# A drain behind every fourth gather of the second expert table

## The chip, the cores and the metric

The kernel runs on one core of a Trainium2 chip. The metric is device time in microseconds (us), the median over several runs. A profile is one further execution, recorded by the hardware profiler; its own time stands beside the median below.

## What is computed

Two transformer-like blocks run one after the other on a sequence of 256 tokens of width 1024, all in float32. The change lies in the last part of the first block, a mixture of very many small experts. Each token is routed, by eight heads that pick 16 experts each, to 128 out of 16384 experts; an expert is one row of a first table `u` and one row of a second table `v`. Cut to that part:

```python
def expert_chunk(args):                     # 128 tokens at a time
    xc, ic, gc = args                       # tokens, expert numbers, gates
    u = jnp.take(u_tab, ic, axis=0)
    a = jnp.einsum('chkd,cd->chk', u, xc)   # one dot product per token and expert
    wgt = gc * jax.nn.gelu(a)
    vv = jnp.take(v_tab, ic, axis=0)
    return jnp.einsum('chk,chkd->cd', wgt, vv)
```

`ic` differs from token to token, so the rows have to be gathered from HBM. The second block (a state-space mixer, a linear recurrence and a feed-forward part) follows on the result.

## The kernel before

The 256 tokens are two tiles of 128, one token on each partition. For a tile the kernel walks through the 128 choices of its tokens: step e (0 to 255 over both tiles) takes, for every token, its choice number e. One step needs two gathers, one from each table, of 128 rows of 1024 float32 numbers, 512 KB each. So there are 512 gathers.

All of them are issued by GpSimd, as indirect DMAs. `gather_u(e)` (line 687) fills one of 5 slots with rows of the first table, `gather_v(e)` (line 701) one of 7 slots with rows of the second. Before it reuses a slot, GpSimd waits: `gather_u(e)` for the flag `dot_ready` of step e - 5, `gather_v(e)` for the flag `pair_summed`, which counts pairs of steps, up to the pair that holds step e - 7. Behind a wait the gather is issued, and its landing raises a semaphore of the slot (`u_full`, `v_full`). The order is written out by hand: step 0 of both tables, step 1 of the first, and then the loop below, in which the first table runs one step ahead.

The other engines consume in order. VectorE takes the dot product of a slot of the first table with the token (`dot_expert`, line 2489), ScalarE turns it into a weight and spreads that on a diagonal matrix (`weigh_expert`, lines 1737 to 1746), and TensorE multiplies the diagonal with the slot of the second table and adds up in PSUM (`sum_expert`, line 1143, two matmuls for each step). Into the same stretch the program folds other work: queries, scores and the routing of the later choices, and projections of the second block's input. The weights for these are loaded by SP on its own queue.

Before that stage GpSimd sets up constants (lines 637 to 675: memsets, iota, small selections and sums) with drains among them; behind the stage it issues a few plain DMAs (lines 718 to 730).

```python
            gather_u(0)
            gather_v(0)
            gather_u(1)
            for e in range(1, TT * EXPERTS):
                if e + 1 < TT * EXPERTS:
                    gather_u(e + 1)
                gather_v(e)
```

Of the kernel before, what the change touches and what calls it, by code (L numbers as in the profile page):

```python
# [244 lines left out]
def pairs(experts):  # L245

    return (experts + 1) // 2


def build(nc, T, out):  # L250

    with ExitStack() as ctx:
# [195 lines left out]
        def flag(name):  # L448

            if name not in S_:  # L450
                S_[name] = sem(name)
            return S_[name]

        def group_wait(eng, name, i):
            g = (name, i)
            eng.wait_ge(bank_full[GROUP_BANK[g]], GROUP_USE[g] + 1)
# [52 lines left out]
        def turn_wait(eng, *u):  # L509

            eng.wait_ge(turned, turn_no[u] + 1)
# [40 lines left out]
        def _(sp):  # L552
            second_halves = []
            for c, (_, w, k0, kt, col, n) in enumerate(CHUNKS):
                b = BEFORE[c]
                if c == FRONT:
# [79 lines left out]
        def _(pool):  # L636
# [41 lines left out]
            def gather_u(e):  # L678

                r, k, slot = e // ROUTE, e % ROUTE, e % NU  # L680
                if e in FIRST_IDX:
                    pool.wait_ge(flag("idx_ready"), FIRST_IDX.index(e) + 1)
                elif e == TOPK or (k == 0 and r):
                    pool.wait_ge(flag("idx_ready"), route_step(e) + len(FIRST_IDX))
                if e >= NU:
                    pool.wait_ge(flag("dot_ready"), e - NU + 1)
                pool.indirect_dma_start(  # L687
                    u_rows[:, slot, :], None, T["peer_u"],
                    bass.IndirectOffsetOnAxis(ap=expert_idx[:, r % 2, k:k + 1], axis=0),
                ).then_inc(u_full[slot], 16)  # L690

            def gather_v(e):

                r, k, slot = e // ROUTE, e % ROUTE, e % NV
                if e >= NV:
                    pool.wait_ge(flag("pair_summed"), pairs(e - NV + 1))
                if e == 0:
                    turn_wait(pool, "m", 1, 0)
                if e == 3:
                    group_wait(pool, "out1", 1)  # L700
                pool.indirect_dma_start(  # L701
                    v_rows[:, slot, :], None, T["peer_v"],
                    bass.IndirectOffsetOnAxis(ap=expert_idx[:, r % 2, k:k + 1], axis=0),
                ).then_inc(v_full[slot], 16)

            gather_u(0)
            gather_v(0)
# [5 lines that stand above are left out]
# [2468 lines left out]
```

## Time and profile before

| what | us |
|---|---|
| median of 3 runs | 1311.55 (1310.23 to 1312.46) |
| span of the profiled execution | 1366.9 |
| GpSimd busy in it | 500.2 |
| TensorE matmuls busy in it | 1199.9 |
| VectorE busy in it | 861.8 |
| ScalarE busy in it | 420.2 |

The profiled execution is 55 us longer than the median; times read from its trace are compared with its own span. A gather's record on GpSimd covers its issue; the movement of its bytes by the 16 DMA engines isn't part of that record and is seen by when the first user of the slot starts.

### The profile page before, as it was taken

The page shows a single profiled execution, that of the slowest core. Times are in us where ns is not written, and L with a number is a line of the kernel's source. Part 1 is how long each engine was busy: PE and PEld are TensorE (multiplying, and loading weights), DVE is VectorE, ACT ScalarE, POOL GpSimd, SP SyncE. Part 2 cuts the span into 40 slices and gives each one's busy share as a digit, 9 for nine tenths or more (in the row PEclk, how much of TensorE's full clock was granted, in tenths as well). Part 3 has the DMA queues.
Part 4 walks back from the last instruction along what each step waited for, and adds up shares of the span by engine and source line. Part 5 has one row for each costly group of instructions (what it writes and reads, how often), then busy time and mean ns, then how long its engine had stood idle before and what let it go on. Part 6 is the DMA issues. An engine that isn't in the chain of part 4 may idle for free. (4 is left out here: it accounts for less than half of the span.)

```text
span 1366.9 us, 14592 instructions
## 1 busy us (share of the span) xinstructions
PE 1199.9 (88%) x4663; PEld 665.4 (49%) x4663; DVE 861.8 (63%) x1765; ACT 420.2 (31%) x1138; POOL 500.2 (37%) x580
## 2 busy tenths in 40 slices
PE   7899888888778978876788889789999999999997
PEld 4676554433344542222345433236544545999443
DVE  2657669574663654776746557679989543676345
ACT  2213334344223343343423324432323311222000
POOL 1000356666665666766666666630000000000000
PEclk9999999999998999999999999999999999999999
DMA  9998789999998999999999999986644444454450
GB/s 358 390 349 326 286 319 339 367 357 367 364 366 300 406 403 405 407 377 364 340 371 353 400 405 409 377 306 233 224 139 148 145 150 156 157 175 145 175 184 31
DMA packets 134303, 405.66 MB, mean 297 GB/s; under 512 B 10153, under 2 KB 11585, under 8 KB 133971
## 3 DMA queue, kind: packets, MB, share of 16 engines
q0 software_dynamic: 75024, 273.19, 53.1%
q1 hardware_dynamic: 57860, 127.48, 25.8%
q10 hardware_dynamic: 1342, 4.06, 0.8%
q8 instruction: 38, 0.62, 0.2%
q14 instruction: 39, 0.31, 0.1%
HBM read 403.12 MB, written 1.05 MB: 296 GB/s over the span
## 5 line engine op out<-in xcount | busy, mean ns | idle before, releaser
L1143 PE MATMUL psum<-gathered,modr 128*128 128x512 f32 x1024 | 505.0, 633 | 130.3 <-DMA gathered<-in_peer_v_dram,expert_idx 49.0
L2489 DVE CUSTOM_DVE_ANT_0 gathered<-gathered,psum 128x1024 f32<-128x1024 f32 x256 | 311.5, 1217 | 202.3 <-DMA gathered<-in_peer_u_dram,expert_idx 153.3
L1143 PEld LDWEIGHTS psum<-gathered,modr 128*128 128x128 f32 x1024 | 190.7, 199 | 404.7 <-issue 284.9
L687 POOL DMA_INDIRECT gathered<-in_peer_u_dram,expert_idx x256 | 244.9, 957 | 240.5 <-DVE expert_idx L1997 144.0
L701 POOL DMA_INDIRECT gathered<-in_peer_v_dram,expert_idx x256 | 242.6, 947 | 169.9 <-remote 73.7
L780 PE MATMUL psum<-featT,weight_ring 128*128 128x128 f32 (+2 forms) x960 | 145.3, 305 | 14.4 <-issue 11.3
L780 PEld LDWEIGHTS psum<-featT,weight_ring 128*128 128x128 f32 x960 | 133.7, 196 | 43.9 <-issue 35.6
L780 PE MATMUL psum<-weight_ring,featT 128*128 128x512 f32 x336 | 147.9, 596 | 1.3 <-ACT featT L1563 0.8
L1737 ACT ACTIVATE gel<-dots 128x1 f32<-128x1 f32 x256 | 51.1, 200 | 255.1 <-issue 128.1
L1746 ACT ACTIVATE modr<-ident,wgt 128x128 f32<-128x128 f32 x256 | 102.8, 402 | 18.5 <-issue 1.1
L780 PEld LDWEIGHTS psum<-weight_ring,featT 128*128 128x128 f32 x336 | 62.6, 190 | 78.8 <-issue 76.6
L1741 ACT ACTIVATE wgt<-gel,expert_gate 128x1 f32<-128x1 f32 x256 | 75.4, 294 | 17.9 <-issue 0.3
L1989 DVE TENSOR_TENSOR work<-work 128x1088 f32<-128x1088 f32 (+5 forms) x87 | 68.6, 801 | 9.6 <-issue 2.8
L725 POOL DMA_DIRECT2D gathered<-in_b_in_dram x6 | 5.3, 942 | 138.6 <-ACT gathered L1585 104.2
L1585 ACT COPY work<-psum 128x128 f32<-128x128 f32 x32 | 8.4, 262 | 81.5 <-remote 44.6
L1978 ACT ACTIVATE work<-work,pack 128x256 f32<-128x256 f32 x28 | 12.7, 500 | 56.8 <-DVE work L1989 56.8
L1989 DVE TENSOR_TENSOR vectors<-weight_ring 128x1024 f32<-128x1024 f32 x14 | 16.5, 1220 | 20.9 <-PE psum L1512 20.9
L1563 ACT COPY featT<-psum 128x512 f32<-128x512 f32 (+1 forms) x24 | 12.4, 554 | 55.0 <-PE psum L752 53.8
L780 PE MATMUL psum<-weight_ring,uT 128*128 128x512 f32 x64 | 28.2, 593 | 1.0 <-ACT gathered L1585 1.0
L1989 DVE TENSOR_TENSOR gathered<-gathered,psum 128x256 f32<-128x256 f32 (+1 forms) x17 | 8.6, 511 | 29.8 <-PE psum L780 24.9
L1473 PE MATMUL psum<-featT,weight_ring 128*128 128x128 f32 x224 | 27.3, 275 | 0.0
L1473 PEld LDWEIGHTS psum<-featT,weight_ring 128*128 128x128 f32 x224 | 26.1, 192 | 0.0
(443 smaller groups left out, 1343.1 us busy)
## 6 DMA issues: line engine op xcount, KB each, us to landing
weight_ring<-in_w_in_dram SPq DMA_DIRECT2D x16, 2048.0 KB
weight_ring<-in_w_up_dram SPq DMA_DIRECT2D x8, 2048.0 KB
weight_ring<-in_w_down_dram SPq DMA_DIRECT2D x8, 2048.0 KB
weight_ring<-in_ada_w_dram SPq DMA_DIRECT2D x5, 2048.0 KB
work<-in_ada_w_dram SPq DMA_DIRECT2D x5, 2048.0 KB, 16.3
weight_ring<-in_peer_wq_dram SPq DMA_DIRECT2D x3, 2048.0 KB
gathered<-in_ada_w_dram SPq DMA_DIRECT2D x2, 2048.0 KB, 14.5
gathered<-in_peer_u_dram,expert_idx POOLq DMA_INDIRECT x256
```

Source lines behind the costliest of these rows:

```text
L687: pool.indirect_dma_start(u_rows[:, slot, :], None, T["peer_u"], bass.IndirectOffsetOnAxis(ap=expert_idx[:, r % 2, k:k + 1], axis=0),).the ...
L701: pool.indirect_dma_start(v_rows[:, slot, :], None, T["peer_v"], bass.IndirectOffsetOnAxis(ap=expert_idx[:, r % 2, k:k + 1], axis=0),).the ...
L780: last = pe.matmul(psum[0:m, bank, 0:n], lhs(k), rhs(k), start=(k == 0), stop=(k == kt - 1))
L1143: mm = pe.matmul(psum[:, SUM_BANK + half, :], diag[:, e % 8, :], v_rows[:, slot, 512 * half:512 * (half + 1)], start=(e % EXPERTS == 0), s ...
L1473: last = pe.matmul(psum[:, UP_BANKS * (n % 2) + bank, at:at + P], a(g, m), b(g), start=(g == 0), stop=(g == 3))
L1563: ins = act.activation(dst, src, func, **kw) if func else act.copy(dst, src)
L1737: act.activation(gel[:, col:col + 1], dots[:, col:col + 1], ACT.Gelu_apprx_tanh)
L1741: act.activation(wgt[:, col:col + 1], gel[:, col:col + 1], ACT.Copy, scale=expert_gate[:, r % 2, k:k + 1])
L1746: act.activation(diag[:, e % 8, :], ident[:, :], ACT.Copy, scale=wgt[:, col:col + 1]).then_inc(flag("diag_full"), 1)
L1978: act.activation(ffT[:, k, :], ffT[:, k, :], ACT.Relu, bias=pk("b_up")[:, k:k + 1])
L1989: return dve.tensor_tensor(o, a, b, op)
L2489: dve.tensor_tensor_reduce(u_rows[:, slot, :], u_rows[:, slot, :], h2_rows[t], 1.0, 0.0, ALU.mult, ALU.add, dots[:, col:col + 1])
```

## The change

Behind every fourth gather of the second table (steps 3, 7, 11 and so on) GpSimd executes a drain. Nothing else in the program differs.

```diff
@@ -702,6 +702,8 @@
                     v_rows[:, slot, :], None, T["peer_v"],
                     bass.IndirectOffsetOnAxis(ap=expert_idx[:, r % 2, k:k + 1], axis=0),
                 ).then_inc(v_full[slot], 16)
+                if e % 4 == 3:
+                    pool.drain()
 
             gather_u(0)
             gather_v(0)
```

## Rows read from the trace of the kernel before

**Rows 1.** The head of the page: the span of the execution.

```profile
span 1366.9 us, 14592 instructions
```

**Rows 2.** Table of stretches: from:to, length, busy us (instructions) of each engine, clock, DMA.

```profile
core 0: us, PE busy (x) PEld busy (x) DVE busy (x) ACT busy (x) POOL busy (x), PEclk, DMA share, GB/s
152.00:907.00 755.00, 614.61 (x1827) 295.48 (x1825) 476.65 (x1150) 280.76 (x874) 487.42 (x512) 0.95 0.98 371
```

**Rows 3.** GpSimd's timeline: start, duration, instruction, [idle time before it <- what ended it].

```profile
326.33 0.94 POOL L701 DMA_INDIRECT gathered<-in_peer_v_dram,expert_idx  x1 [3.23 <-remote]
327.57 0.94 POOL L687 DMA_INDIRECT gathered<-in_peer_u_dram,expert_idx  x1 [0.30 <-issue]
328.82 0.94 POOL L701 DMA_INDIRECT gathered<-in_peer_v_dram,expert_idx  x1 [0.30 <-issue]
...
335.05 0.94 POOL L687 DMA_INDIRECT gathered<-in_peer_u_dram,expert_idx  x1 [0.30 <-issue]
...
343.76 0.94 POOL L701 DMA_INDIRECT gathered<-in_peer_v_dram,expert_idx  x1 [0.30 <-issue]
```

**Rows 4.** Line 687, all instructions: ns min/median/max, first and last start in us.

```profile
L687 POOL DMA_INDIRECT gathered<-in_peer_u_dram,expert_idx x256: 934/941/1484, 152.0 to 902.3; - x128
```

**Rows 5.** The chain that ended last, at the stage's end: start, duration, what.

```profile
904.90 7.71 DMA gathered<-in_peer_v_dram,expert_idx
...
912.66 2.00 PE psum L1143 x4
```

**Rows 6.** GpSimd's waits in the stage: us in total, times, longest.

```profile
POOL gathered L701 <- remote: 73.7, 29, 4.2
POOL gathered L687 <- issue: 72.9, 228, 1.4
POOL gathered L701 <- issue: 67.5, 215, 2.3
POOL gathered L701 <- PE psum L1143: 28.7, 12, 8.7
POOL gathered L687 <- DVEq L2491: 23.6, 27, 4.4
```

**Rows 7.** VectorE's timeline in the stretch of rows 3: dot products.

```profile
333.05 1.22 DVE L2489 CUSTOM_DVE_ANT_0 gathered<-gathered,psum 128x1024 f32<-128x1024 f32 x1 [2.10 <-DMA gathered<-in_peer_u_dram,expert_idx]
...
341.39 1.22 DVE L2489 CUSTOM_DVE_ANT_0 gathered<-gathered,psum 128x1024 f32<-128x1024 f32 x1 [1.31 <-DMA gathered<-in_peer_u_dram,expert_idx]
```

**Rows 8.** GpSimd's timeline in its opening; drains before lines 649, 661, 667 and 671.

```profile
2.07 0.14 POOL L644 IOTA iota<- 128x16 f32 x1
2.15 1.11 POOL L647 MEMSET inv_freq<- 128x1 f32 x32
3.47 0.29 POOL L649 TENSOR_SCALAR_AFFINE_SELECT ident<-ident 128x128 f32<-128x128 f32 x1 [0.21 <-issue]
...
4.21 0.28 POOL L657 TENSOR_SCALAR_AFFINE_SELECT causal<-causal 128x128 f32<-128x128 f32 x1
4.62 1.14 POOL L661 MEMSET quarter_rows<- 1x128 f32 x4
...
6.70 0.65 POOL L667 TENSOR_TENSOR meta_rows<-meta_rows,ident 128x32 f32<-128x32 f32 x2
7.49 0.31 POOL L671 COPY w_gates<-meta_rows 128x4 f32<-128x4 f32 x2
```

**Rows 9.** GpSimd's groups by line: busy us, mean ns | idle us before.

```profile
L687 POOL DMA_INDIRECT gathered<-in_peer_u_dram,expert_idx x256 | 244.9, 957 | 240.5 <-DVE expert_idx L1997 144.0 <-issue 72.9 <-DVEq L2491 23.6
L701 POOL DMA_INDIRECT gathered<-in_peer_v_dram,expert_idx x256 | 242.6, 947 | 169.9 <-remote 73.7 <-issue 67.5 <-PE psum L1143 28.7
```

**Rows 10.** GpSimd's timeline around 500 us: the first and last of four long gathers.

```profile
492.05 1.34 POOL L687 DMA_INDIRECT gathered<-in_peer_u_dram,expert_idx  x1 [0.70 <-DVEq L2491]
...
507.61 1.33 POOL L687 DMA_INDIRECT gathered<-in_peer_u_dram,expert_idx  x1 [0.74 <-DVEq L2491]
```

## The prediction

> **What bounds the kernel now.** I read the head of the page first, then the table of three stretches, GpSimd's timeline and waits, and VectorE's timeline beside it. The profiled execution lasts 1366.9 us [rows 1], and the part that the change touches is the expert stage: the 512 gathers of the two expert tables lie between 152 and 907 us, 755 us of the span, and there the DMA engines are 0.98 busy at 371 GB/s while TensorE and VectorE are busy for 615 and 477 us [rows 2]. So bytes set the pace on the whole, and GpSimd, which issues them, is close behind with 487 us [rows 2].
>
> How close is seen in its timeline. Where nothing stops it, GpSimd starts a gather every 1.245 us (from 328.82 to 343.76 are 12 steps, 14.94 us), of which 0.94 is the instruction and 0.30 a gap before the next [rows 3]. 511 such steps make 636 us; the stage takes 752.9 us from the first start at 152.0 [rows 4] to the last at 904.90 [rows 5]. The rest is waiting. The list of its waits has 73.7 + 28.7 us in front of gathers of the second table (the slot must have been summed by TensorE) and 23.6 us in front of those of the first (the slot must have been read by VectorE), 68 times together; less the 0.30 us that each gap has anyway that is 106 us. The 443 gaps called "issue", 140.4 us, hold 7.5 us over their 0.30 [rows 6]. So GpSimd has about 113 us of pauses.
>
> Otherwise it runs ahead of the data. A gather of the first table started at 327.57 us (expert 59, counted in program order on both engines) is used by VectorE at 333.05, at its landing, 5.48 us later; the one started at 335.05, eighth in its unbroken series, at 341.39, 6.34 us later [rows 3, 7]. At 1.245 us a step some five gathers are under way at any time. That overlap is what keeps the DMA engines full.
>
> The stage ends with GpSimd's last gather: the chain of waits goes from its start at 904.90 over 7.71 us to the landing, and to TensorE's last sums at 912.66 [rows 5]. What follows, some 455 us, doesn't use these gathers, and I leave it as it is.
>
> **The change, step by step.** One instruction is added, 64 times (experts 3, 7, ... 255), behind the gather of the second table. Nothing is removed or reordered. Behind the 64th GpSimd waits for TensorE's last sum anyway, so 63 count. Queued behind each are the next gathers: first that of the first table for the expert after next, then one of the second, and so on. VectorE's dot product and TensorE's sum of these experts wait for them, and ScalarE between the two. The DMAs of SP and ScalarE don't pass through GpSimd.
>
> What does a drain wait for? The trace has drains only in GpSimd's opening, between memsets and small operations. Without one, instructions there overlap: the memsets of line 647 start at 2.15, before the operation of line 644 ends at 2.07 + 0.14 [rows 8]. With one, the next starts behind the end: 4.21 + 0.28 is 4.49, and line 661 starts at 4.62; 6.70 + 0.65 is 7.35, and line 671 starts at 7.49 [rows 8]. So a drain holds the next instruction until the one ahead is finished, and 0.13 or 0.14 us more. A gather has two ends, and no row shows a drain behind one:
>
> - the end of its record, 0.94 us behind its start. A gap of 0.30 us already follows it, more than the 0.14 that a drain takes. The cost is then between 0 and 0.21 us, the longest gap behind a drained operation (line 647 ends at 3.26, line 649 starts at 3.47) [rows 8]; 63 x 0.21 = 13 us of GpSimd's time at most, less than its 113 us of pauses. A gain isn't excluded; it is a rival below.
> - the landing of its rows, 5.48 to 7.71 us behind its start [rows 3, 5, 7].
>
> I take the landing. The opening's drains stand where the next instruction reads or overwrites what the one ahead wrote (line 667 adds onto meta_rows), so what a drain gives there is finished writing, not a finished issue; and a gather's rows are not there when its record ends: their first user starts 4.5 us later (333.05 against 327.57 + 0.94) [rows 3, 7].
>
> The record ends 0.94 us behind the gather's start, and what moves the bytes goes on behind it [rows 3, 7]. The Trainium skill has a rule that speaks against my choice: by "GPSIMD Engine Reference", section 2.1 (Instruction dispatch), an instruction of this engine that neither reads nor writes a tensor by itself is complete when each of the engine's cores has signalled. By that rule the drain would be over with the record, and the sum would be that of the first end; no row here shows which holds.
>
> The price by the landing: today the step behind the eighth gather of a group is 1.245 us. With the drain it is the time from that gather's start to its landing, and GpSimd's next start takes the place of VectorE's in the row: 6.34 us for an eighth gather behind a pause, which the last of each group will be. The drain itself adds 0.13. That is 6.34 + 0.13 - 1.245 = 5.23 us more per group, and 63 x 5.23 = 329 us.
>
> From this comes off what GpSimd now waits for slots. The tightest case behind a drain is the last gather of a group: it needs the sum of a pair of experts whose later rows came fourth in the group before. They landed some 5 us before that group's drain ended, and the sum is wanted 7 x 1.245 = 8.7 us after it: 13.7 us for what takes TensorE and its neighbours a few us, with a longest pause of 8.7 us in the rows and a mean of 126 / 68 = 1.9 [rows 6]. Also the consumers get 15 us for four experts where they have 752.9 / 64 = 11.8 now. So I strike all 113 us, and the 4 us that 752.9 - 636 - 113 leaves (longer instructions, rounding). The last landing is 7.71 - 6.34 = 1.4 us nearer. The sum: 329 - 117 - 1 = 211 us, or per group 7 x 1.245 + 6.34 + 0.13 = 15.2 us instead of 11.8. The profiled execution would go from 1366.9 to 1578 us.
>
> The median of the runs shown is 1311.55 us, 55 us under the profiled execution, and no row says where those 55 us lie. Carried over unchanged, 211 us give 1522; scaled by 1311.55 / 1366.9, 203 us give 1514. I say 1520 us.
>
> The bounds: with 5.48 us and a drain that takes nothing itself, 63 x (5.48 - 1.245) - 117 = 150 us; with 7.71 + 0.13, 63 x 6.60 - 117 = 299 us. On the median that is 1461 to 1610. I start the range at 1455, since the first of these, scaled as above, is 144 us.
>
> **The rivals.**
>
> - The drain ends with the record. For it: the gap of 0.30 us between gathers is the same throughout, as if GpSimd already finished one before it starts the next [rows 3]. Against it: what drains do in the opening [rows 8]. At most 13 us are added to GpSimd and taken out of its pauses: 1311.5 us, and 2 us more if a sixth of them falls where it runs without a pause. That the instruction does nothing at all gives the same time and is counted here.
> - Faster. Some gathers take up to 1.48 us instead of the median 0.94 [rows 4]; all of them together take 244.9 + 242.6 us [rows 9], 6 us over 512 x 0.941. Four of the long ones stand close together from 492 to 508 us, each behind a pause for VectorE [rows 10]. If they are GpSimd waiting for room in its queue, a drain that sees the queue emptied makes that room during a pause: 1311.5 - 6 = 1306 us. It decides only if a drain costs under 6 / 63 = 0.1 us, so only where it doesn't wait for the landing.
> - The landing is waited for, and the pauses stay. For it: TensorE has other work in this stage, 615 us with the sums [rows 2], which gets no shorter. Then 329 us are added and nothing comes off: 1311.5 + 329 = 1640 us. Against it: the 13.7 us above, longer than any pause in the rows [rows 6].
>
> **How the numbers follow.** The landing with swallowed pauses 0.85, nearly all of it within its bounds; the record's end 0.11; the gain 0.02; the landing with the pauses left 0.02. The predicted time is the first case's, 1520 us; the range 1455 to 1610 is its bounds and leaves out the other three, 0.15 in sum. A measurement of this kernel can tell a difference of about 0.2%, 2.6 us, from none. Slower by more than that: 0.85 + 0.02, and 0.01 out of the record's end, 0.88. Within: the other 0.10. Faster: 0.02.
>
> **What would show it.** In the profile after, GpSimd's timeline has groups of eight gathers 1.245 us apart and then a gap of 5 to 6 us, 63 times, that ends with the landing of the eighth. The waits for TensorE and VectorE in front of gathers all but vanish. The DMA engines' share in the stage falls from 0.98 to about 0.98 x 11.8 / 15.2 = 0.76; the stage from first start to last start is near 752.9 + 212 = 965 us; what follows it is as long as now. The forecast is wrong if the gap behind the eighth is 0.3 to 0.5 us (the record's end), or if the 68 pauses stand beside the drains. If the gaps are there but shorter or longer, the landing was mis-sized, by 63 times the difference.

## The result and the profile after

With the drains the kernel takes 1667.8 us (median, 1664.6 to 1667.9); beside it on the same chip the kernel before takes 1311.0 us. The ratio is 1.271 (95% interval 1.270 to 1.273), 356.8 us more. The forecast was slower, 1520 us with a range of 1455 to 1610: the direction and the wait for the landing came out, the size didn't.

The head of the page and the table of stretches of the kernel after (columns as in [rows 2]: from:to, length, busy us of each engine, granted clock, DMA share, GB/s):

```profile
span 1666.1 us, 14656 instructions
...
150.00:1201.00 1051.00, 720.10 (x1831) 329.45 (x1830) 482.54 (x1152) 286.48 (x874) 484.35 (x512) 0.83 0.75 266
1201.00:1666.00 465.00, 450.38 (x2104) 272.91 (x2103) 301.92 (x434) 97.78 (x185) 7.00 (x9) 0.99 0.46 159
```

The expert stage is 1051 us long where [rows 2] had 755, with the same 512 gathers on GpSimd and the same bytes; the DMA engines' share fell from 0.98 to 0.75. What follows the stage is about as long as it was (465 us against 460). GpSimd's timeline in it (start, duration, instruction, idle time before it and what ended it), two whole groups but for the middle:

```profile
412.41 0.93 POOL L687 DMA_INDIRECT gathered<-in_peer_u_dram,expert_idx  x1 [6.09 <-issue]
413.65 0.94 POOL L701 DMA_INDIRECT gathered<-in_peer_v_dram,expert_idx  x1 [0.30 <-PE psum L1145]
...
419.86 0.93 POOL L687 DMA_INDIRECT gathered<-in_peer_u_dram,expert_idx  x1 [0.30 <-issue]
421.10 0.94 POOL L701 DMA_INDIRECT gathered<-in_peer_v_dram,expert_idx  x1 [0.31 <-issue]
428.49 0.93 POOL L687 DMA_INDIRECT gathered<-in_peer_u_dram,expert_idx  x1 [6.46 <-issue]
...
437.19 0.93 POOL L701 DMA_INDIRECT gathered<-in_peer_v_dram,expert_idx  x1 [0.30 <-issue]
```

This is the picture that the forecast drew: eight gathers 1.24 us apart (412.41 to 421.10 are seven steps, 8.69 us), then nothing for 6.46 us. All 63 gaps are there; the median step from the eighth start to the next is 7.53 us, the mean 7.77. GpSimd's waits (us in total, times, longest), to be read against [rows 6]:

```profile
POOL gathered L687 <- issue: 434.5, 245, 11.6
POOL gathered L701 <- issue: 68.6, 225, 0.3
POOL gathered L687 <- DVEq L2493: 52.6, 9, 7.0
POOL gathered L701 <- PE psum L1145: 9.4, 31, 0.3
```

Gathers of the second table now wait 0.3 us at most, so the slots hold nothing up any more. The gaps behind the drains are booked on "issue", and nine of them on VectorE, whose signal happened to come nearby. VectorE itself shows what the gap waits for. Its dot product of the seventh gather of the group above, started at 419.86, begins at the landing:

```profile
426.19 1.22 DVE L2491 CUSTOM_DVE_ANT_0 gathered<-gathered,psum 128x1024 f32<-128x1024 f32 x1 [0.32 <-DMA gathered<-in_peer_u_dram,expert_idx]
```

The records of the DMA packets show the end of the eighth, started 1.24 us later: its last packet is over at 427.03, and GpSimd starts again at 428.49, 1.47 us behind it. It is so in all 63 gaps: the step from the eighth start to the next lies between 7.01 and 12.54 us, but the next start comes 1.42 to 1.67 us behind the group's last packet every time. In five of the 63 a transfer of another queue was under way there, with packets moving in the gap and on behind the restart; GpSimd started 1.46 to 1.67 us behind its own last packet there too. So a drain waits for the gathers of GpSimd and not for all traffic of the DMA engines.

### The profile page after: what moved, and what is told of

Its sections match the earlier page's. It is cut to its first block, busy times and chain, and to the rows that moved or that the text cites. A ratio compares the mean times of both kernels' runs of the same rounds, so it can differ in the third digit from the quotient of the medians.

```text
span 1666.1 us, 14656 instructions
## 1 busy us (share of the span) xinstructions
PE 1305.7 (78%) x4663; PEld 698.7 (42%) x4663; DVE 868.0 (52%) x1765; ACT 425.7 (26%) x1138; POOL 497.1 (30%) x580
## 3 DMA queue, kind: packets, MB, share of 16 engines
HBM read 403.12 MB, written 1.05 MB: 243 GB/s over the span
## 4 chain that ended last, share of the span: by engine, by line
PE 38%; DMA 27%; POOL 15%; issue 8%; DVE 5%; POOLq 4%; DVEq 1%; ACT 1%; ACTq 0%; SPq 0%
PE psum L782 14%; DMA gathered<-in_peer_v_dram,expert_idx 12%; DMA gathered<-in_peer_u_dram,expert_idx 12%; POOL gathered L687 9%; PE psum L1145 7%; POOL gathered L701 6%; PE psum L1475 5%; PE psum L1514 5%; POOLq L706 4%; DVE gathered L2491 2%; DMA work<-in_ada_w_dram 1%; DMA weight_ring<-in_w_in_dram 1%; DMA vectors<-in_attn_out_g_dram 1%; PE psum L875 1%; PE psum L805 1%
## 5 line engine op out<-in xcount | busy, mean ns | idle before, releaser
L1145 PE MATMUL psum<-gathered,modr 128*128 128x512 f32 x1024 | 606.4, 737 | 333.5 <-DMA gathered<-in_peer_v_dram,expert_idx 318.9
L1145 PEld LDWEIGHTS psum<-gathered,modr 128*128 128x128 f32 x1024 | 218.5, 230 | 674.5 <-DMA gathered<-in_peer_v_dram,expert_idx 470.4
L687 POOL DMA_INDIRECT gathered<-in_peer_u_dram,expert_idx x256 | 240.6, 940 | 630.3 <-issue 434.5
L1565 ACT COPY featT<-psum 128x512 f32<-128x512 f32 (+1 forms) x24 | 12.4, 554 | 55.0 <-PE psum L754 53.8
L1514 PE MATMUL psum<-weight_ring,work 128*128 128x512 f32 x56 | 25.3, 592 | 0.0
L1991 DVE TENSOR_TENSOR modr<-weight_ring 128x1024 f32<-128x1024 f32 x14 | 16.5, 1218 | 14.1 <-PE psum L1514 14.1
```

The lines of the kernel that those rows point to most:

```text
L687: pool.indirect_dma_start(u_rows[:, slot, :], None, T["peer_u"], bass.IndirectOffsetOnAxis(ap=expert_idx[:, r % 2, k:k + 1], axis=0),).the ...
L1145: mm = pe.matmul(psum[:, SUM_BANK + half, :], diag[:, e % 8, :], v_rows[:, slot, 512 * half:512 * (half + 1)], start=(e % EXPERTS == 0), s ...
L1514: last = pe.matmul(psum[:, PRODUCT_BANK[i], :], a(g), b(g), start=(n == 0 and g == 0), stop=(n == WINOGRAD - 1 and g == 1))
L1991: return dve.tensor_tensor(o, a, b, op)
```

## The experiments

### The kernel before, once more

> The kernel before, unchanged, to see which of its two times its trace belongs to. The forecast took the profiled execution (1366.9 us) as the runs shown (1311 us) plus a constant. If profiling itself costs 55 us, the time is near 1311 us and the span of its trace near 1367 us again. If the execution of the first trace was an odd one, the span is near 1311 us too, and the rows say where 55 us went: in the expert stage (from the first gather's start to the last about 698 us instead of 753), or beside it (753 again).

Measured: 1312.2 us, and a span of 1310.4. So profiling by itself doesn't add 55 us, and the execution of [rows 1 to 10] was an odd one: every timed run of the kernel before lies between 1310 and 1315 us. The head of the new page, the stage and two stretches that can be set beside the first trace:

```profile
span 1310.4 us, 14592 instructions
...
152.00:847.00 695.00, 598.47 (x1823) 281.67 (x1822) 478.50 (x1147) 284.64 (x870) 491.79 (x512) 0.99 1.02 403
200.00:250.00 50.00, 47.09 (x170) 25.51 (x169) 41.05 (x115) 22.70 (x72) 36.55 (x40) 0.97 1.01 398
250.00:300.00 50.00, 42.30 (x128) 19.26 (x127) 38.60 (x88) 23.63 (x67) 37.60 (x40) 1.00 1.03 409
```

The same two stretches in the first trace:

```profile
200.00:250.00 50.00, 44.01 (x156) 23.75 (x155) 36.43 (x101) 21.25 (x69) 32.24 (x34) 0.93 0.95 347
250.00:300.00 50.00, 43.13 (x134) 22.13 (x133) 33.03 (x92) 18.82 (x58) 33.62 (x36) 0.93 0.98 366
```

The stage has 403 GB/s and a DMA share of 1.02 in the usual execution, 371 and 0.98 in the first trace [rows 2]. (The share is the sum of the packets' times over 16 engines; it is over 1 where packets overlap.) The lines of the first and last gathers (ns min/median/max, first and last start; first table, then second) give its length, 845.0 - 152.3 = 692.7 us instead of 752.9:

```profile
L687 POOL DMA_INDIRECT gathered<-in_peer_u_dram,expert_idx x256: 932/937/1924, 152.3 to 842.5; - x128
...
L701 POOL DMA_INDIRECT gathered<-in_peer_v_dram,expert_idx x256: 932/937/1836, 153.8 to 845.0; - x128
```

So all of the 55 us lay in the expert stage (and 4 us more, since the work behind it takes 465.4 us here and 462.0 there). Of the 692.7 us, 636 are GpSimd's 511 steps; pauses and long instructions are 56.5 us, not 117. TensorE's weight loads for its sums stood idle 28 us longer in the first trace. Its group there, then once more (busy us, mean ns | idle us before):

```profile
L1143 PEld LDWEIGHTS psum<-gathered,modr 128*128 128x128 f32 x1024 | 190.7, 199 | 404.7 <-issue 284.9
```

```profile
L1143 PEld LDWEIGHTS psum<-gathered,modr 128*128 128x128 f32 x1024 | 180.6, 192 | 376.3 <-DMA gathered<-in_peer_v_dram,expert_idx 219.2
```

The causes booked in the two can't be compared: the first trace holds 4158 of the DMAs' semaphore signals where the second has 9768, so a wait can stand under "issue" or "remote" there for want of the signal or of its sender. That the 73.7 us under "remote" in [rows 6] are a wait for TensorE follows from the program, which has GpSimd wait there for nothing else. The lengths of its pauses, and their sum of 113 us, don't depend on it. TensorE's granted clock in the stage was lower too, 0.95 [rows 2] against 0.99. Whether that is a cause of the longer execution or goes with it isn't shown, and why it was longer stays open.

### A wait for the landing in place of the drain

```diff
+                if e % 4 == 3:
+                    pool.wait_ge(v_full[slot], 16 * (e // NV + 1))
```

> Instead of the drain GpSimd waits, at the same 64 places, for the semaphore of that gather's landing. Theory A (the drain is a wait for the landing and little more): as the changed kernel, 1668 us, or less by what the drain takes on top; the trace after shows GpSimd starting 1.42 to 1.67 us behind the last packet, where VectorE's start follows its last packet by about 0.9, so at most 63 x 0.6 = 38 us less: 1630 to 1668 us. Theory B (the drain waits for something else and later, such as all traffic of the DMA engines): clearly under 1600 us.

Measured: 1620.75 us (ratio to before 1.236, 1.233 to 1.238). GpSimd's timeline near the same time:

```profile
427.13 0.94 POOL L701 DMA_INDIRECT gathered<-in_peer_v_dram,expert_idx  x1 [0.30 <-issue]
434.42 0.94 POOL L687 DMA_INDIRECT gathered<-in_peer_u_dram,expert_idx  x1 [6.36 <-DMA gathered<-in_peer_v_dram,expert_idx]
```

The gap is now put down to the gather by name, and it is nearly as long as behind a drain. The wait alone costs 308 us of the 357. Theory B, under 1600 us, falls; with the constant delay behind the last packet, seen above, theory A holds: the drain waits for the landing. The time is 9 us under the least that theory A gave, since the wait lets GpSimd start earlier, against the drain, than the 0.6 us assumed: 0.63 us behind the last packet in the median, and a drain 1.47. The drain takes 47 us more than the wait, 0.75 us each.

### The wait, and then the drain

```diff
+                if e % 4 == 3:
+                    pool.wait_ge(v_full[slot], 16 * (e // NV + 1))
+                    pool.drain()
```

> The wait for the landing and then the drain, so that the drain finds nothing under way. Its own cost alone: with 0.13 us as in the opening of the program, wait4 plus 8 us; with 0.5 us, wait4 plus 32 us. If it then comes out at the time of the changed kernel (1668 us), the drain's own overhead is the whole difference between wait4 and the change.

Measured: 1687.0 us (1.285, 1.281 to 1.288), 66 us over the wait alone: 1.05 us for a drain that finds no transfer under way. The line of the drain (ns min/median/max, first and last start) says where most of it is:

```profile
L707 POOLq DRAIN  x64: 609/691/799, 168.5 to 1232.4; - x64
```

Its record lasts 0.69 us with the awaited gather landed. Both of the sizes expected, 0.13 and 0.5 us, were too small. The time is 19 us above that of the change, not at it; that some of the drain's own time runs beside the landing in the change would explain it, but isn't shown.

### Two drains in a row

```diff
+                if e % 4 == 3:
+                    pool.drain()
+                    pool.drain()
```

> Two drains in a row at the same places. The drain behind a landed gather cost 1.05 us in wait4_drain, where 0.13 was forecast. If that is a fixed price of a drain, 63 x 0.7 to 1.05 = 44 to 66 us over the changed kernel: 1712 to 1734 us. If it is a price for tidying up behind the gathers issued since the last drain (the start behind the last packet is 1.5 us late after eight gathers, 1.9 after sixteen), the second drain finds none and costs 0.05 to 0.2 us: 1671 to 1681 us.

Measured: 1675.2 us (1.277, 1.275 to 1.279), 7.4 us over the change (the kernel before took 1311.9 beside it, 1311.0 beside the change), 0.12 us for each second drain. Its line:

```profile
L707 POOLq DRAIN  x64: 47/47/47, 167.5 to 1216.9; - x64
```

A drain that finds nothing to do costs what the opening's drains cost [rows 8]. So the 0.7 us of the experiment before aren't a fixed price of a drain; they belong to the gathers that were issued since the last one. What the drain does in that time isn't seen.

### The drain at half and at double the distance

```diff
+                if e % 8 == 7:
+                    pool.drain()
```

> The drain behind every eighth gather of the second table instead of every fourth, 32 instead of 64. The net price in the change is 356.8 / 63 = 5.66 us per drain. If the price is the same for each, 1311 + 31 x 5.66 = 1487 us. If each drain costs its whole gap, 6.5 us, and swallows only the pauses near it: 1311 + 31 x 6.5 less 0 to 57 us, 1455 to 1513 us. In the trace GpSimd's pauses for slots are back in the second half of each group of sixteen if the second holds with few swallowed.

```diff
+                if e % 2 == 1:
+                    pool.drain()
```

> The drain behind every second gather of the second table, 128 of them, groups of four gathers. If the price is the lost overlap, a group takes 3 x 1.245 + about 5.7 (start to last packet of a fourth gather) + 0.6 for the wait + the drain's own time. With a drain's own time of 0.85 us whatever stands before it, 10.9 us per group, and 128 groups 1395 us where the stage now takes 693: 2014 us. If the own time is 0.45 us and 0.05 for each gather, 0.65 us: 10.7 per group, 1988 us, and the start follows the last packet by 1.25 us instead of 1.5. If the price per drain were that of the change, 5.66 us each: 1312 + 127 x 5.66 = 2031 us.

Measured: 1499.9 us with 32 drains (1.143, 1.141 to 1.146) and 1964.6 us with 128 (1.500, 1.495 to 1.506). The same net price for each drain gave 1487 and 2031; the price falls as they come closer together: 188 / 31 = 6.05 us, 356.8 / 63 = 5.66, 653 / 127 = 5.14. With 32 drains the time lies in the range of the other case (1455 to 1513). With 128 it lies below all three cases (1988, 2014 and 2031): from the start of a group's last gather to its last packet were 5.51 us in the mean where some 5.7 had been assumed, and 128 x 0.19 = 24 us is what the nearest case has too much. One group's end of each, 32 drains first:

```profile
415.86 0.94 POOL L701 DMA_INDIRECT gathered<-in_peer_v_dram,expert_idx  x1 [0.30 <-PE psum L1145]
424.06 0.93 POOL L687 DMA_INDIRECT gathered<-in_peer_u_dram,expert_idx  x1 [7.26 <-issue]
```

```profile
417.75 0.94 POOL L701 DMA_INDIRECT gathered<-in_peer_v_dram,expert_idx  x1 [0.30 <-issue]
424.52 0.94 POOL L687 DMA_INDIRECT gathered<-in_peer_u_dram,expert_idx  x1 [5.83 <-DVEq L2493]
```

Over all groups, worked out from GpSimd's starts and from the records of the DMA packets (128 packets of 4096 bytes make a gather):

| kernel | gathers per group | step behind the last, us, median (mean) | start behind its last packet, us, median |
|---|---|---|---|
| wait for the landing | 8 | 6.58 (6.95) | 0.63 |
| 128 drains | 4 | 6.61 (6.77) | 1.26 |
| 64 drains (the change) | 8 | 7.53 (7.77) | 1.47 |
| 64 pairs of drains | 8 | 7.61 (7.90) | 1.56 |
| wait, then drain | 8 | 7.86 (8.13) | 1.81 |
| 32 drains | 16 | 8.36 (8.97) | 1.87 |

Against the plain wait (run behind groups of eight alone) a drain is later by 0.63, 0.84 and 1.24 us behind 4, 8 and 16 gathers: these three points fit about 0.4 us and 0.05 for each gather. The forms "a fixed own time" and "a price per drain" both fall. With 32 drains the pauses for slots don't come back, which was the sign of the second case there: outside of the drains four gaps over 0.35 us are left, where the usual execution of the kernel before has 56 at the places that aren't behind a fourth gather.

### Waiting for an earlier gather

The same wait, but for the gather of the second table one expert earlier, and two experts earlier, so that two and four gathers stay under way.

```diff
+                if e % 4 == 3:
+                    pool.wait_ge(v_full[(e - 1) % NV], 16 * ((e - 1) // NV + 1))
```

> As wait4, but GpSimd waits for the landing of the gather of the second table one expert earlier, two gathers back, so that two stay under way. wait4 cost 308 us, with a step of 6.58 us (median) behind the eighth gather. Theory A (the price of a fence is the overlap that it throws away): the awaited gather started 2 x 1.245 = 2.5 us earlier, so the step is some 4.1 to 4.4 us, 2.5 less: 1621 - 63 x 2.5 = 1463 us. Theory B (each stop of GpSimd costs the same, however much stays under way): as wait4, near 1620 us.

```diff
+                if e % 4 == 3:
+                    pool.wait_ge(v_full[(e - 2) % NV], 16 * ((e - 2) // NV + 1))
```

> The wait for the landing two experts earlier, four gathers back. Theory A: 5 us less than wait4 in each step, about 1.6 us instead of 6.6, against the 1.245 that it takes anyway; with the deeper queue of the kernel before (landings 7 us behind the start) the step is up to 2.3 us: 1312 to 1370 us. Theory B: near 1620 us.

Measured: 1470.4 us (1.121, 1.119 to 1.123) and 1320.9 us (1.0075, 1.0058 to 1.0092). The steps behind the last gather are 4.17 and 1.53 us in the median. The two timelines, one gather of the second table back and then two:

```profile
412.88 0.94 POOL L701 DMA_INDIRECT gathered<-in_peer_v_dram,expert_idx  x1 [0.30 <-issue]
416.93 0.94 POOL L687 DMA_INDIRECT gathered<-in_peer_u_dram,expert_idx  x1 [3.11 <-DMA gathered<-in_peer_v_dram,expert_idx]
```

```profile
416.57 0.94 POOL L701 DMA_INDIRECT gathered<-in_peer_v_dram,expert_idx  x1 [0.30 <-issue]
422.84 0.94 POOL L687 DMA_INDIRECT gathered<-in_peer_u_dram,expert_idx  x1 [5.33 <-DMA gathered<-in_peer_v_dram,expert_idx]
```

GpSimd meets a wait at the same 64 places in all of these. With nothing left under way that costs 308 us, with two gathers 158, with four 9; the second pair of rows is one of the few long stops that the mean of 2.13 us holds. The 9 us aren't the stops alone: the 63 steps grew by 63 x (2.13 - 1.245) = 56 us, but the stage, 705.2 us from first start to last, by 12.5, since the new waits took the place of most of the 56.5 us of pauses that the kernel before has anyway. Theory A (the price is the overlap thrown away) holds, and theory B (each stop costs the same) falls.

## Why the prediction was wrong in size

- **What bounds the kernel.** Right: the bytes, with GpSimd close behind. In the usual execution it is even clearer: a DMA share of 1.02 at 403 GB/s.
- **What a drain waits for.** Right: the landing. The wait in its place reproduces 308 of the 357 us. The reading of the opening [rows 8], that a drain there gives finished writing, carried over to gathers. The rival that the drain ends with the record would have left 1312 us, and it is out. So is the use made in it of a rule of the Trainium skill ("GPSIMD Engine Reference", section 2.1, Instruction dispatch): the rule tells when an instruction is complete, not what a drain waits for, and here that isn't the end of the gather's record, 0.94 us behind its start.
- **The landing, 6.34 us.** Somewhat low. With the plain wait the step was 6.58 us in the median, 6.95 in the mean, since some landings came late (the longest gap is 10.6 us). The row was one good case, and the sum needs the mean: 63 x (6.95 - 6.34) = 38 us too little.
- **"The drain itself adds 0.13."** Wrong: 7.77 - 6.95 = 0.82 us in the mean, 63 x 0.69 = 43 us too little. The row from the opening was right for a drain right behind another (0.12 us); behind eight gathers a drain takes some 0.8 us beyond the wait for the landing.
- **"So I strike all 113 us, and the 4 us".** The mechanism was right: the pauses are all but gone in every run where GpSimd waits for the last gather (four at most over 0.35 us). The size was wrong, because the pauses were those of an odd execution. The usual one has 56.5 us of pauses and long instructions, of which 2 are left after: 54.5 struck instead of 117, 62 us too little. This is the largest term, and the prediction had the sign of it in hand: it noted that the profiled execution was 55 us longer than the median, that no row said where those lie, and then carried the difference over unchanged. It had to ask whether the 55 us were part of the 113. With 113 + 4 - 55 = 62 us struck, the same sum gives 329 - 62 - 1 = 266 us, 1578 us, inside its own range. The three terms, 62, 43 and 38 us, are 143 of the 148 us by which the forecast was short. The range missed because its bounds moved the landing and at most 0.13 us for the drain; the 117 us were in both of them as they stood.
- **The sum again, with what was measured:** 63 x (7.77 - 1.245) = 411 us, less 54.5, is 356.5; measured 356.8. This closes by construction, since the 54.5 come from the lengths of the same two stages. What it does show is that the stage, 1049.1 us (150.6 to 1199.8) less 692.7, holds the whole difference: 356.4.
- **The other rivals.** "The pauses stay" named the nearest time, 1640 us, by the wrong road, so by luck: the pauses went, and there were fewer to go. The faster rival, room in GpSimd's queue, is out with the landing. Gathers over 1.0 us are 48 in the usual execution of the kernel before and 17 after, some 8 us in all; the first trace has 22, so that the drain made them rarer isn't shown.
- **What would show it.** Groups of eight and 63 gaps: seen. The gap of 5 to 6 us: 6.6 in the median, and the text had said that a longer one means a landing mis-sized by 63 times the difference; about half of the difference is the drain's own time instead. DMA share 0.76: it is 0.75, by luck. The stage grew more than forecast, and with packets as long as in the usual execution the share would be 1.02 x 692.7 / 1049.1 = 0.67; but the mean record of a gather's packet went from 164 to 183 ns. The stage near 965 us: 1049.

## What to carry to other kernels

A fence (here a drain or a wait that keeps further transfers from being issued) cost in this kernel the overlap that it threw away, and not the stop itself: the time from the last issue to its landing, less one issue step, times the number of fences, less the pauses that it took the place of, and for a drain its own time besides. Waiting for a transfer four places back cost 9 us where waiting for the last cost 308. Before waiting time of a trace is credited against a new wait, compare the traced execution with the timed runs: if it is longer, the surplus may be the very pauses that are about to be credited. And a drain on the engine that issues gathers was here a wait for their landing and 0.75 us more, so where only an order has to be kept, wait on the semaphore of the one transfer that matters.

## What the runs showed of the hardware that was not expected

- A drain on GpSimd behind eight gathers, the last of them landed, still has a record of 0.69 us; one right behind another takes 0.047 us in its record and 0.12 us in the kernel's time. Over 4, 8 and 16 gathers its delay beyond a plain wait was 0.63, 0.84 and 1.24 us.
- The record of a drain that has to wait is no measure of the wait: in the kernel after the 64 drains have a median record of 12.4 us, longer than the gap of 6.6 us that they make, since the record begins while gathers ahead are still being issued:

```profile
L706 POOLq DRAIN  x64: 8127/12392/17382, 159.5 to 1194.8; - x64
```

- TensorE's granted clock in the expert stage was lower with the gaps, 0.83 after against 0.99 in the usual execution before; both are means over its two levels, 2.4 and 1.2 GHz. The trace has 61 stretches at the lower level in the stage after, 356 us in all, and 5 before, 20.5 us. TensorE's matmuls were busy for 0.69 of the stage after and 0.86 before. The mean matmul of line 1143 (1145 after) went from 617 to 737 ns. That cost nothing visible, as GpSimd never waited for TensorE over 0.3 us.
- One execution of an unchanged kernel was 55 us (4%) longer than all its timed runs, within one stage.
